# A convolution copy one tile sooner, the branch mean at tile 27, and one centring per tile, in a sparse-attention stage

## The chip, the cores and the metric

The kernel runs on one core of a Trainium2 chip. The metric is the device time of one execution in microseconds; the time before is the median of three runs. One execution was also profiled.

## The reference, cut to what matters

The program is a hybrid layer (a sparse attention with a convolution branch beside it, a cross attention, a gated feed-forward) followed by a state-space layer and a forgetting attention with their feed-forwards, for 512 tokens of width 1024 in float32. The change lies in the first part, where the attention and the branch are computed:

```python
    a_out = dsa_attention(q, k, v, qi, ki, wi)          # 8 heads of 64, 128 keys kept per query
    ga, gg = jnp.split(glu, 2, axis=-1)
    u = ga * jax.nn.sigmoid(gg)                          # 512 tokens x 512 channels
    u = causal_dwconv(u, conv_b_w, conv_b_b)             # 31 taps per channel
    b_out = jax.nn.silu(layernorm(u, ln_b_g, ln_b_b))
    x = x + jnp.concatenate([a_out, b_out], axis=-1) @ w_out
```

`layernorm` subtracts the mean over the 512 channels, then divides by the root of the mean square plus a small constant.

## The kernel before, in words

Each engine has its own program, written out by hand in the order in which it is to run; semaphores tie them together. There is no scheduler: an instruction that waits holds all that stands behind it on its engine.

The attention stage is 32 tiles, n = 8 c + t: c is one of 4 pairs of heads, t picks one of 2 heads and one of 4 query blocks of 128. For tile n TensorE makes scores (`scores`, three matmuls into a bank of FOUR, three tiles ahead), VectorE their negated maximum (`negative_max`, L2466, two tiles ahead), ScalarE the exponentials (`exponentials`, L800, two tiles ahead), TensorE turns the result (`turn`, L1798, into a bank of ACC), ScalarE copies its high part (`turned_high`, L815, into PTH), VectorE makes the low remainder (`turned_low`, L2500, into PTL, one tile behind), and TensorE multiplies with the values (`values`, L1755 to L1757, into O). In the last pair VectorE also divides each tile by its sum (`divide`, L2471 and L2473), before `turn`. In the other pairs the sums are turned on TensorE (`turn_sums`, L1891), copied by ScalarE at the next pair's t = 3 (`sums_copied`, L884, into RBs) and multiplied into the output by VectorE (`scaled_out`, L2489); `scaled_high` (L889) and `scaled_low` (L2495) split the product. `turn` of a tile with t = 3 waits for that copy.

The convolution runs beside it. Channels are in four blocks CV[0] to CV[3]. Block 0 is made by VectorE, one tap per tile (`taps`, L2373). Blocks 1 to 3 are made by TensorE as chunks of 32 steps, 4 steps in each of 8 tiles (`convolve_beside`), with diagonal weight tiles that GpSimd builds (`diagonals`, L1295), into the PSUM bank ST. There is one such bank: in the ninth tile ScalarE copies it out in four pieces and adds the bias (`convolved`, L897), and the first step of the next chunk waits for that copy (`conv_pe`). So the copies stand at tiles 8, 17 and 26.

Then comes the normalisation of the branch. TensorE sums all channels into ST (`branch_mean`, L1919, at tile 28), VectorE subtracts the mean from the four blocks (L2583, at tile 29), ScalarE squares them (`branch_square`, L903: tiles 30 and 31, and two after the loop), and GpSimd adds the squares (L1266, L1268). TensorE's `column_sums` after the first unit of the output projection wait for the last sum. The projection (`first_projected`, then `unit`, L1626, L1627, L1632) begins when tile 30's remainder is made. Its weights are loaded by SyncE into RAW, rounded by ScalarE (L627, WH) and their remainder made by GpSimd (L1255, WL), which frees the buffer for the next load.

Of the kernel before, what the change touches and what calls it, by code (L numbers as in the profile page):

```python
# [19 lines left out]
ALU = mybir.AluOpType  # L20
# [3 lines left out]
P = 128  # L24
# [10 lines left out]
BCH = 4  # L35
# [13 lines left out]
CONV_TILES = 8  # L49
CONV_CHUNKS = 3  # L50
# [76 lines left out]
def build_program(nc, A, out):  # L127
    ctx = ExitStack()
    with ctx:
        first = (nc.sbuf_base + 127) // 128 * 128  # L130

        def at(name, shape, dt, offset):
            return nc.alloc_sbuf_tensor_at(name, shape, dt, offset=first + offset)

        def bank(name):
            return ctx.enter_context(nc.psum_tensor(name, [P, 512], F32))

        def sem(name):
            return ctx.enter_context(nc.semaphore(name))
# [72 lines left out]
        CV = [at(f"CV{c}", [P, T], F32, (184320, 152576, 34816, 36864)[c]) for c in range(BCH)]  # L212
# [102 lines left out]
        def column(name, i):  # L315
# [6 lines left out]
        ST = bank("ST")  # L322
# [40 lines left out]
        u_ready, u_hi, u_lo, wc_hi, diag_ready, diag_used, conv_pe, conv_done, mean_sum, centred, ln_scaled, branch_hi, branch_lo = (  # L363
            sem(n) for n in ("u_ready", "u_hi", "u_lo", "wc_hi", "diag_ready", "diag_used",
                             "conv_pe", "conv_done", "mean_sum", "centred", "ln_scaled", "branch_hi", "branch_lo"))
# [256 lines left out]
        def _(act):  # L622
# [13 lines left out]
            def square_free(norm, c):  # L636
                if not isinstance(c, int) or SQUARES[norm] + c >= 2:
                    act.wait_ge(sq_used, SQUARES[norm] + c - 1)
# [179 lines left out]
            def out_high(kind, c, half=None):  # L818

                for m in range(1 + (kind == "cross")) if half is None else (half,):  # L820
                    chunk = bass.ds(2 * c + m if kind == "cross" else c, 1)
                    high_out((O, ST)[m], OUT[kind][0][:, chunk, :],
                             VALUES[kind] + (2 * c + m + 1 if kind == "cross" else 8 * c + 8))
# [43 lines left out]
            def high_out(bank_, to, k):  # L867

                act.wait_ge(pv_done, k)
                act.activation(to, bank_[:], ACT.Copy).then_inc(o_hi, 1)  # L870
# [8 lines left out]
            def sums_copied(kind, c, bank_):  # L879

                act.wait_ge(sums_turned, LATE[kind] + c + 1)
                if c:
                    act.wait_ge(o_scaled, LATE[kind] + c)
                act.activation(RB[kind][:], bank_[:], ACT.Copy).then_inc(sums_in, 1)  # L884
# [15 lines left out]
            def branch_square(c):  # L900
                act.wait_ge(centred, c + 1)
                square_free("ln", c)
                act.activation(SQ[:, c % 2, :], CV[c][:], ACT.Square).then_inc(sq_ready, 1)  # L903

            def attend_sparse():
                for t in range(2):
                    exponentials("sparse", t, t)
                for c in range(4):
                    for t in range(8):
                        n = 8 * c + t  # L910
                        if n + 2 < 32:
                            exponentials("sparse", n + 2, t + 2)
                        if t == 3 and c:
                            sums_copied("sparse", c - 1, TT[1])
                        turned_high("sparse", c, t)
                        if t == 4 and c:
                            scaled_high("sparse", c - 1)
                        if n % (CONV_TILES + 1) == CONV_TILES and n < CONV_CHUNKS * (CONV_TILES + 1):
                            convolved(n // (CONV_TILES + 1))
                        if n >= 30:  # L920
                            branch_square(n - 30)
                for c in range(2, BCH):
                    branch_square(c)
                out_high("sparse", 3)

            attend_sparse()

            def silu_branch(c):
# [192 lines left out]
            with act.Fori(0, 4) as i:  # L1121
                for b in range(2):
                    c = 2 * i + b
# [490 lines left out]
        def _(pe):  # L1614
# [307 lines left out]
            def attend_sparse():  # L1922
                for t in range(3):
                    scores("sparse", 0, 0, t)
                for c in range(4):
                    b = c % 2
                    for t in range(8):
                        n = 8 * c + t
                        if t + 3 < 8:
                            scores("sparse", c, b, t + 3)  # L1930
                        elif c < 3:
                            scores("sparse", c + 1, 1 - b, t - 5)
                        convolve_beside(n)
                        turn("sparse", c, t)
                        if t >= TB:
                            values("sparse", c, b, 0, BLOCKS["sparse"][t - TB])
                        elif c:
                            if t == 2:
                                turn_sums("sparse", c - 1, TT[1])
                            values("sparse", c - 1, 1 - b, 1, BLOCKS["sparse"][t])  # L1940
                        if n == 28:
                            branch_mean()

            pe.sem_inc(t_ready, 4)
# [258 lines left out]
        def _(dve):  # L2203
# [350 lines left out]

            dve.sem_inc(pt_lo, 2)

            def attend_sparse():
                def low_tile(n):
                    turned_low(n, n % 8, n % TB, keys("sparse", n % 8) // P)

                for t in range(2):
                    negative_max("sparse", t, t)
                for c in range(4):
                    for t in range(8):
                        n = 8 * c + t
                        if c == LAST["sparse"]:
                            divide("sparse", n, t)
                        if t == 0 and c:
                            inverse("sparse", c - 1)
                        if n + 2 < 32:  # L2570
                            negative_max("sparse", n + 2, t + 2)
                        if n:
                            low_tile(n - 1)
                        if t == 3 and c:
                            scaled_out("sparse", c - 1)
                        if t == 5 and c:
                            scaled_low("sparse", c - 1)
                        if n + 8 < CONVW:
                            taps(n + 8, n + 9)
                        if n == 29:  # L2580
                            dve.wait_ge(mean_sum, 1)
                            for k in range(BCH):
                                dve.scalar_tensor_tensor(CV[k][:], ST[:], -1.0 / (BCH * P), CV[k][:], ALU.mult, ALU.add)\  # L2583
                                   .then_inc(centred, 1)
                low_tile(31)
                out_low("sparse", 3)

# [444 lines left out]
            for j, to in enumerate((KT, VT)):  # L3032
                with dve.Fori(0, 4) as i:
                    for s in range(2):
                        c = 2 * i + s
                        dve.wait_ge(unit_done, START["kv"] + j * 8 + c + 1)
                        dve.tensor_tensor(to[:, bass.ds(c, 1), :], ACC[s][:], RS[:], ALU.mult).then_inc(unit_out, 1)
                    c = i + 4 * j
# [114 lines left out]
```

## Time and profile before

| | |
|---|---|
| median of 3 runs | 2074.13 us (2071.26 to 2075.82) |
| profiled execution, own time | 2074.17 us |
| its span | 2072.4 us |
| TensorE busy | 1968.3 us, 95% |
| VectorE, GpSimd, ScalarE busy | 1058.3, 1060.5, 743.8 us |
| mean granted clock of TensorE | 0.99 |

The own time is that of the execution the profile was taken of, and the span is the part of it that the profile covers. Times inside the profile are microseconds from the span's start; PE is TensorE's matmuls, PEld its weight loads, DVE VectorE, ACT ScalarE, POOL GpSimd, SP SyncE. The sparse stage's tiles run from about 188 to 286 us.

### The profile page before, as it was taken

The numbers are of one execution on the slowest core, as the hardware profiler recorded it, in microseconds if no ns is written. First come the engines' busy times: TensorE is split into PE (matmuls) and PEld (weight loads), VectorE is DVE, ScalarE is ACT, GpSimd is POOL, SyncE is SP. The second block draws the span as 40 slices with busy tenths as digits, with TensorE's granted clock in tenths as the row PEclk, the third lists the DMA queues.
The fourth block names the chain that finished last, engine by engine and source line by source line (L and its number), as shares of the span: only waits on it lengthen the run. The fifth ranks groups of instructions, "written<-read, shape, count | busy, mean of one in ns | idle before, by whom it ended". The sixth has DMA issues, their size and how long they took to land.

```text
span 2072.4 us, 31378 instructions
## 1 busy us (share of the span) xinstructions
PE 1968.3 (95%) x10733; PEld 1623.0 (78%) x10733; DVE 1058.3 (51%) x1640; ACT 743.8 (36%) x1263; POOL 1060.5 (51%) x591
## 2 busy tenths in 40 slices
PE   7989889899999999889999999999998899999997
PEld 5679867778887887667778888887878788888886
DVE  6798745835786786797442213232137724222132
ACT  4335444433213224354432222233237732222223
POOL 5576627536756645681554444456445264444442
PEclk9999999999999999999999999999999999999999
DMA  4334003143333332101233333334346333333332
GB/s 137 77 112 117 21 26 102 41 92 91 101 92 91 102 91 79 44 2 28 86 91 102 91 102 96 95 93 102 100 108 148 88 102 94 94 97 96 96 95 87
DMA packets 345028, 181.87 MB, mean 88 GB/s; under 512 B 28527, under 2 KB 336103, under 8 KB 344935
## 3 DMA queue, kind: packets, MB, share of 16 engines
q1 hardware_dynamic: 343872, 179.91, 31.3%
q8 instruction: 55, 0.90, 0.2%
q10 hardware_dynamic: 1062, 0.75, 0.1%
q14 instruction: 39, 0.31, 0.0%
HBM read 162.73 MB, written 2.10 MB: 80 GB/s over the span
## 4 chain that ended last, share of the span: by engine, by line
PE 57%; issue 12%; POOL 9%; DVE 7%; POOLq 6%; ACT 3%; DVEq 2%; SPq 2%; DMA 1%; ACTq 0%
PE ACC L1626 16%; PE ACC L1632 16%; PE ACC L1627 16%; POOL WL L1255 6%; POOLq L1269 2%; POOLq L1480 1%; POOLq L1468 1%; PE ACC L1798 1%; PE ST L2098 1%; POOL GC L1479 1%; ACT WH L627 1%; PE O L1757 1%; PE O L1755 1%; POOL GT L1467 1%; PE ST L1755 1%
## 5 line engine op out<-in xcount | busy, mean ns | idle before, releaser
L1255 POOL TENSOR_TENSOR WL<-RAW,WH 128x1024 fp32r<-128x1024 f32 (+1 forms) x292 | 692.3, 2373 | 733.4 <-ACT WH L627 677.3
L1626 PE MATMUL ACC<-PH,WH 128*128 128x512 f32 x1248 | 492.7, 395 | 8.1 <-DVE PL L2207 2.7
L1627 PE MATMUL ACC<-PL,WH 128*128 128x512 f32 x1248 | 487.3, 391 | 0.0
L627 ACT ACTIVATE WH<-RAW 128x1024 fp32r<-128x1024 f32 (+1 forms) x292 | 301.0, 1032 | 452.3 <-PE ACC L1632 403.6
L1626 PE MATMUL ACC<-QH,WH 128*128 128x512 f32 (+1 forms) x1136 | 429.6, 382 | 14.0 <-ACT WH L627 7.4
L1627 PE MATMUL ACC<-QL,WH 128*128 128x512 f32 (+1 forms) x1136 | 425.4, 379 | 0.0
L1632 PE MATMUL ACC<-PH,WL 128*128 128x512 f32 x1248 | 312.9, 393 | 0.0
L1626 PEld LDWEIGHTS ACC<-PH,WH 128*128 128x128 f32 x1248 | 235.1, 188 | 66.4 <-issue 4.9
L1632 PE MATMUL ACC<-QH,WL 128*128 128x512 f32 (+1 forms) x1136 | 270.0, 378 | 7.2 <-POOL WL L1255 3.9
L1632 PEld LDWEIGHTS ACC<-PH,WL 128*128 128x128 f32 x1248 | 234.5, 188 | 52.7 <-issue 3.6
L1627 PEld LDWEIGHTS ACC<-PL,WH 128*128 128x128 f32 x1248 | 235.1, 188 | 48.7 <-issue 1.0
L1626 PEld LDWEIGHTS ACC<-QH,WH 128*128 128x128 f32 x1136 | 214.8, 189 | 63.1 <-issue 9.2
L1627 PEld LDWEIGHTS ACC<-QL,WH 128*128 128x128 f32 x1136 | 214.8, 189 | 38.9 <-issue 0.2
L1632 PEld LDWEIGHTS ACC<-QH,WL 128*128 128x128 f32 x1136 | 205.3, 188 | 49.3 <-POOL WL L1255 5.9
L3024 DVE TENSOR_TENSOR X<-X,ACC 128x512 f32 x48 | 33.0, 688 | 216.3 <-PE ACC L1632 216.3
L3014 DVE TENSOR_TENSOR H<-ACC,RS 128x512 f32<-128x512 f32 x64 | 44.3, 692 | 149.1 <-PE ACC L1632 148.6
L1268 POOL TENSOR_TENSOR SSQ<-SSQ,SQ 128x512 f32<-128x512 f32 x51 | 75.0, 1470 | 68.1 <-ACT SQ L634 63.8
L875 ACT ACTIVATE QH<-H 128x512 f32 (+1 forms) x54 | 34.1, 632 | 158.2 <-DVE H L3016 128.3
L2500 DVE TENSOR_TENSOR PTL<-ACC,PTH 128x128 fp32r<-128x128 f32 (+2 forms) x112 | 53.3, 476 | 36.2 <-ACT PTH L815 35.8
L815 ACT ACTIVATE PTH<-ACC 128x128 fp32r<-128x128 f32 (+2 forms) x112 | 47.9, 428 | 56.6 <-PE O L1757 37.0
L875 ACT ACTIVATE PH<-H 128x512 f32 (+1 forms) x32 | 20.2, 632 | 128.3 <-DVE H L3016 128.3
L2836 DVE TENSOR_TENSOR QL<-H,QH 128x512 f32 x54 | 37.4, 693 | 49.5 <-ACT QH L875 49.5
(448 smaller groups left out, 2565.0 us busy)
## 6 DMA issues: line engine op xcount, KB each, us to landing
RAW<-in_mlp_w_dram SPq DMA_DIRECT2D x128, 512.0 KB, 4.0
RAW<-in_w_gate_dram SPq DMA_DIRECT2D x22, 512.0 KB, 3.8
RAW<-in_w_up_dram SPq DMA_DIRECT2D x22, 512.0 KB, 3.8
RAW<-in_w_in_dram SPq DMA_DIRECT2D x16, 512.0 KB, 3.9
RAW<-in_w_down_dram SPq DMA_DIRECT2D x16, 512.0 KB, 4.1
RAW<-in_ssm_w_glu_dram SPq DMA_DIRECT2D x16, 512.0 KB, 3.8
RAW<-in_w_kvf_dram SPq DMA_DIRECT2D x16, 512.0 KB, 4.0
RAW<-in_w_out_dram SPq DMA_DIRECT2D x16, 256.0 KB, 2.8
```

The source lines that it names most:

```text
L627: act.activation(WH[:, s, 0:kc], RAW[:, s, 0:kc], ACT.Copy).then_inc(w_hi, 1)
L815: act.activation(parts(kind, t // TB)[0][:, first:first + kb, qb * P:(qb + 1) * P], TT[t % 2][:, 0:kb * P].rearrange("p (k q) -> p k q", q ...
L875: act.activation(hi[:, bass.ds(k, 1), :], to, ACT.Copy).then_inc(hid_hi, 1)
L1255: pool.tensor_tensor(WL[:, s, 0:kc], RAW[:, s, 0:kc], WH[:, s, 0:kc], ALU.subtract).then_inc(w_lo, 1)
L1268: pool.tensor_tensor(SSQ[:], SSQ[:], SQ[:, s, :], ALU.add).then_inc(sq_used, 1)
L1269: pool.drain()
L1626: pe.matmul(ACC[s][:, 0:n], WH[:, s, k, :], xh[:, k, :], start=(k == 0), stop=False)
L1627: pe.matmul(ACC[s][:, 0:n], WH[:, s, k, :], xl[:, k, :], start=False, stop=False)
L1632: mm = pe.matmul(ACC[s][:, 0:n], WL[:, s, k, :], xh[:, k, :], start=False, stop=(k == kc - 1))
L1755: pe.matmul(out, ah, bh, start=first, stop=False)
L2500: dve.tensor_tensor(pair[1][to], TT[t % 2][:, 0:kb * P].rearrange("p (k q) -> p k q", q=P), pair[0][to], ALU.subtract).then_inc(pt_lo, 1)
L3014: dve.tensor_tensor(h[:], ACC[s][:], RS[:], ALU.mult).then_inc(unit_out, 1)
```

## The change

Three things. ScalarE copies the convolution result in the eighth tile of a chunk (tiles 7, 16 and 25), right behind the last convolution matmuls. TensorE sums the mean at tile 27 instead of 28. VectorE centres one block in each of tiles 28 to 31 instead of four at tile 29; the squares on ScalarE begin at tile 29 and go one per tile, and the fourth stands behind the copy of the attention output (`out_high`).

```diff
--- before.py
+++ after.py
@@ -915,13 +915,12 @@
                         turned_high("sparse", c, t)
                         if t == 4 and c:
                             scaled_high("sparse", c - 1)
-                        if n % (CONV_TILES + 1) == CONV_TILES and n < CONV_CHUNKS * (CONV_TILES + 1):
+                        if n % (CONV_TILES + 1) == CONV_TILES - 1 and n < CONV_CHUNKS * (CONV_TILES + 1):
                             convolved(n // (CONV_TILES + 1))
-                        if n >= 30:
-                            branch_square(n - 30)
-                for c in range(2, BCH):
-                    branch_square(c)
+                        if n >= 29:
+                            branch_square(n - 29)
                 out_high("sparse", 3)
+                branch_square(3)
 
             attend_sparse()
 
@@ -1938,7 +1937,7 @@
                             if t == 2:
                                 turn_sums("sparse", c - 1, TT[1])
                             values("sparse", c - 1, 1 - b, 1, BLOCKS["sparse"][t])
-                        if n == 28:
+                        if n == 27:
                             branch_mean()
 
             pe.sem_inc(t_ready, 4)
@@ -2554,6 +2553,11 @@
 
             dve.sem_inc(pt_lo, 2)
 
+            def centre(k):
+                dve.wait_ge(mean_sum, 1)
+                dve.scalar_tensor_tensor(CV[k][:], ST[:], -1.0 / (BCH * P), CV[k][:], ALU.mult, ALU.add)\
+                   .then_inc(centred, 1)
+
             def attend_sparse():
                 def low_tile(n):
                     turned_low(n, n % 8, n % TB, keys("sparse", n % 8) // P)
@@ -2577,11 +2581,8 @@
                             scaled_low("sparse", c - 1)
                         if n + 8 < CONVW:
                             taps(n + 8, n + 9)
-                        if n == 29:
-                            dve.wait_ge(mean_sum, 1)
-                            for k in range(BCH):
-                                dve.scalar_tensor_tensor(CV[k][:], ST[:], -1.0 / (BCH * P), CV[k][:], ALU.mult, ALU.add)\
-                                   .then_inc(centred, 1)
+                        if n >= 28:
+                            centre(n - 28)
                 low_tile(31)
                 out_low("sparse", 3)
 
```

How it moves instructions, at three places. Lines behind the edits are shifted by one or two in the changed kernel. The first is ScalarE at tiles 7 to 10: E and E2sparse are exponentials, PTH copied transposes, CV_132 block 1 of the convolution.

```order
 L800 ACTIVATE E,SUMF<-FOUR,NMX 128x256
 L815 ACTIVATE PTH<-ACC 128x4x128
-L800 ACTIVATE E2sparse,SUMF<-FOUR,NMX 128x384
-L815 ACTIVATE PTH<-ACC 128x128
 L897 ACTIVATE CV_132<-ST,VEC 64x256
 L897 ACTIVATE CV_132<-ST,BSW 64x256 x2
 L897 ACTIVATE CV_132<-ST,VEC 64x256
+L800 ACTIVATE E2sparse,SUMF<-FOUR,NMX 128x384
+L815 ACTIVATE PTH<-ACC 128x128
 L800 ACTIVATE E3sparse,SUMF<-FOUR,NMX 128x512
 L815 ACTIVATE PTH<-ACC 128x2x128
```

The four copies moved ahead of the exponentials of tile 10 and of tile 8's copied transposes; the other two chunks are moved in the same way.

The second is TensorE from the transposes of tile 27 on: FOUR<-KSH, KSL, SEL are the scores of tile 31, ACC<-CST,E the transposes of tile 28, O its values, ST<-CV the mean. Before:

```order
L1798 MATMUL ACC<-CST,E3sparse 128x128 x4
L1779 MATMUL FOUR<-KSH,AQ_79 128x512
L1780 MATMUL FOUR<-KSL,AQ_79 128x512
L1781 MATMUL FOUR<-SEL,PAIR 128x512
L1798 MATMUL ACC<-CST,E 128x128
L1755 MATMUL O<-PTH,VSH 128x512
L1756 MATMUL O<-PTL,VSH 128x512
L1757 MATMUL O<-PTH,VSL 128x512
L1919 MATMUL ST<-CV_131,CST 128x512
L1919 MATMUL ST<-CV_132,CST 128x512
L1919 MATMUL ST<-CV_133,CST 128x512
L1919 MATMUL ST<-CV_134,CST 128x512
```

The same place after the change:

```order
L1797 MATMUL ACC<-CST,E3sparse 128x128 x4
L1918 MATMUL ST<-CV_131,CST 128x512
L1918 MATMUL ST<-CV_132,CST 128x512
L1918 MATMUL ST<-CV_133,CST 128x512
L1918 MATMUL ST<-CV_134,CST 128x512
L1778 MATMUL FOUR<-KSH,AQ_79 128x512
L1779 MATMUL FOUR<-KSL,AQ_79 128x512
L1780 MATMUL FOUR<-SEL,PAIR 128x512
L1797 MATMUL ACC<-CST,E 128x128
L1754 MATMUL O<-PTH,VSH 128x512
L1755 MATMUL O<-PTL,VSH 128x512
L1756 MATMUL O<-PTH,VSL 128x512
```

The mean stands ahead of tile 31's scores and of tile 28's transposes and values.

The third is VectorE from tile 28's remainder to the division of tile 30 or 31: REC and E are a division, NMX a maximum, PTL a remainder, QL the low part of the scaled output, CV_131 to CV_134 the blocks that are centred. Before:

```order
L2500 TENSOR_TENSOR PTL<-ACC,PTH 128x128
L2495 TENSOR_TENSOR QL<-OFs,QH 128x512
L2583 SCALAR_TENSOR_TENSOR CV_131<-ST,CV_131 128x512
L2583 SCALAR_TENSOR_TENSOR CV_132<-ST,CV_132 128x512
L2583 SCALAR_TENSOR_TENSOR CV_133<-ST,CV_133 128x512
L2583 SCALAR_TENSOR_TENSOR CV_134<-ST,CV_134 128x512
L2471 RECIPROCAL REC<-SUM 128x1
L2473 TENSOR_SCALAR E2sparse<-E2sparse,REC 128x384
```

From tile 28's centring on, after the change:

```order
L2558 SCALAR_TENSOR_TENSOR CV_131<-ST,CV_131 128x512
L2470 RECIPROCAL REC<-SUM 128x1
L2472 TENSOR_SCALAR E<-E,REC 128x256
L2465 TENSOR_REDUCE NMX<-FOUR 128x1
L2499 TENSOR_TENSOR PTL<-ACC,PTH 128x128
L2494 TENSOR_TENSOR QL<-OFs,QH 128x512
L2558 SCALAR_TENSOR_TENSOR CV_132<-ST,CV_132 128x512
L2470 RECIPROCAL REC<-SUM 128x1
L2472 TENSOR_SCALAR E2sparse<-E2sparse,REC 128x384
L2499 TENSOR_TENSOR PTL<-ACC,PTH 128x2x128
L2558 SCALAR_TENSOR_TENSOR CV_133<-ST,CV_133 128x512
L2470 RECIPROCAL REC<-SUM 128x1
```

The first centring, with its wait for the mean, now stands ahead of tile 29's division and maximum; two centrings stand ahead of tile 30's division instead of four, and a third ahead of tile 31's.

## Rows read from the trace of the kernel before

**Rows 1.** The page, part 1: busy time, share of the span, instructions.

```profile
PE 1968.3 (95%) x10733; PEld 1623.0 (78%) x10733; DVE 1058.3 (51%) x1640; ACT 743.8 (36%) x1263; POOL 1060.5 (51%) x591
```

**Rows 2.** TensorE by stretches: length, busy time, granted clock, DMA share, GB/s.

```profile
214.30:220.00 5.70, 5.67 (x25) 0.51 0.00 0
220.00:240.60 20.60, 20.15 (x153) 1.00 0.16 39
243.80:247.10 3.30, 3.30 (x18) 0.50 0.03 5
271.90:278.00 6.10, 6.08 (x14) 0.50 0.00 0
284.60:288.10 3.50, 3.38 (x13) 0.52 0.00 0
401.80:407.00 5.20, 5.19 (x31) 1.00 0.01 3
```

**Rows 3.** Timeline of TensorE: start, us, instruction, idle before and its releaser.

```profile
214.33 0.55 PE L1755 MATMUL ST<-UH,DGH 128*128 128x256 f32 x1 [2.10 <-ACT CV L897]
...
243.01 0.36 PE L1755 MATMUL ST<-UH,DGH 128*128 128x256 f32 x1 [2.42 <-ACT CV L897]
...
271.92 1.09 PE L1798 MATMUL ACC<-CST,E3sparse 128*128 128x128 f32 x4 [2.75 <-issue]
...
283.64 0.55 PE L1798 MATMUL ACC<-CST,E2sparse 128*128 128x128 f32 x3 [2.40 <-DVE E2sparse L2473]
...
401.76 0.44 PE L1798 MATMUL ACC<-CST,E 128*128 128x128 f32 x2 [1.78 <-DVE E L2473]
```

**Rows 4.** Who writes tile CV: count, ns minimum/median/maximum, first and last start.

```profile
L2373 DVE SCALAR_TENSOR_TENSOR CV<-U,VEC,CV x30: 739/1054/2387, 173.0 to 256.4; 128x512 f32<-128x512 f32 x30
...
L897 ACT ACTIVATE CV<-ST,VEC x6: 471/478/488, 212.2 to 270.3; 64x256 f32<-64x256 f32 x6
```

**Rows 5.** Timeline of ScalarE around its copies: start, us, instruction, idle before.

```profile
208.89 0.60 ACT L815 ACTIVATE PTH<-ACC 128x512 fp32r<-128x512 f32 x1 [1.71 <-PE ACC L1798]
...
223.09 0.60 ACT L884 ACTIVATE RBs<-ACC 128x512 f32<-128x512 f32 x1
...
239.28 0.28 ACT L815 ACTIVATE PTH<-ACC 128x128 fp32r<-128x128 f32 x1 [0.99 <-PE O L1757]
...
268.40 0.49 ACT L815 ACTIVATE PTH<-ACC 128x384 fp32r<-128x384 f32 x1 [1.33 <-PE O L1757]
```

**Rows 6.** Timeline of VectorE, tiles 11 and 12, and TensorE behind it.

```profile
223.73 0.69 DVE L2489 TENSOR_TENSOR OFs<-O,RBs 128x512 f32<-128x512 f32 x1 [0.39 <-ACT RBs L884]
224.33 1.10 DVE L2373 SCALAR_TENSOR_TENSOR CV<-U,VEC,CV 128x512 f32<-128x512 f32 x1
...
226.89 0.48 PE L1755 MATMUL O<-PTH,VSH 128*128 128x512 f32 x1
```

**Rows 7.** Timeline of the mean and the end of the stage, three engines.

```profile
272.66 0.78 PE L1779 MATMUL FOUR<-KSH,AQ 128*128 128x512 f32 x1
...
275.86 4.63 PE L1919 MATMUL ST<-CV,CST 128*128 128x512 f32 x8
...
276.34 0.62 ACT L889 ACTIVATE QH<-OFs 128x512 fp32r<-128x512 f32 x1
...
277.06 0.69 DVE L2495 TENSOR_TENSOR QL<-OFs,QH 128x512 fp32r<-128x512 f32 x1 [0.29 <-ACT QH L889]
...
280.54 2.48 DVE L2583 SCALAR_TENSOR_TENSOR CV<-ST,CV 128x512 f32<-128x512 f32 x4 [2.78 <-PE ST L1919]
...
285.78 0.79 PE L1626 MATMUL ACC<-QH,WH 128*128 128x512 f32 x1
```

**Rows 8.** Timeline behind the stage: GpSimd, ScalarE, TensorE's weight load.

```profile
289.77 1.27 POOL L1268 TENSOR_TENSOR SSQ<-SSQ,SQ 128x512 f32<-128x512 f32 x1 [0.16 <-issue]
...
290.43 0.60 ACT L870 ACTIVATE QH<-O 128x512 fp32r<-128x512 f32 x1 [1.54 <-PE O L1757]
...
293.07 1.09 PEld L1646 LDWEIGHTS ST<-CST,SSQ 128*128 128x128 f32 x8
```

## The prediction, made before the changed kernel was run

> **What bounds the kernel now.** I read the page first, then TensorE's granted clock by stretches, then its idle time with the releaser named, then the engines around each hole. TensorE is busy for 95% of the span, nothing else comes near [rows 1], so a change pays only where TensorE stands still or runs slowly. The stage in question is the sparse attention with the convolution beside it, some 100 of the 2072.4 us. Between 220.0 and 240.6 TensorE is busy 20.15 of 20.60 us at clock 1.00: there it is the limit. But it stands still four times for over 2 us: 2.10 before 214.33 and 2.42 before 243.01, both released by ScalarE's convolution copy, 2.75 before 271.92, and 2.40 before 283.64, released by a VectorE division [rows 3]. After each of them stands a stretch at about half of the full clock (0.50 to 0.52, that is 1.2 of 2.4 GHz): 5.7, 3.3, 6.1 and 3.5 us [rows 2]. Half the clock means that half of such a stretch is lost. A hole of 1.78 us before 401.76 [rows 3] was followed by clock 1.00 [rows 2]. So a hole has two prices, its own length and what the clock loses behind it; shortened far enough, it saves both.
>
> The sum is made against the profiled execution: 2074.17 us, span 2072.4. The median of the runs is 2074.13, so one number serves for both.
>
> **Part A, first copy, at tile 7 instead of 8.** The copy is four instructions of 0.48 us each [rows 4], 1.95 us with the steps between them. Now it comes behind the exponentials of tile 10 and the copy of tile 8's transposes, and TensorE, whose next convolution writes the same bank, waits until 214.33. After the change it follows tile 7's transposes copy, which ends at 208.89 + 0.60 = 209.49 [rows 5]. All convolution matmuls of the chunk stand ahead of those transposes on TensorE, so the copy waits for nothing: it ends at 211.45. TensorE arrives at 214.33 - 2.10 = 212.23. The hole is gone: 2.10, and with it half of 5.7, so 2.85 [rows 2, 3]; 4.95 at most. What is late next? The exponentials of tile 10 and tile 8's copy, pushed back by 1.2 and 0.3 us (estimates from where they stand), are wanted by TensorE only at tile 10, over 3 us later. Then the chain through VectorE: from the end of the copied sums, 223.09 + 0.60 [rows 5], to the value matmuls of tile 12 at 226.89 [rows 6], it is 3.2 us: scaling 0.69, a tap 1.10, a maximum, a remainder. TensorE, 4.95 earlier, would reach its sums-dependent transposes at about 219.5, and ScalarE has the sums copied at 219.6 to 220.1, as the tap before is short or long. Plus 3.2 is 222.8 to 223.3, against 226.89: 3.6 to 4.1. I take **3.8**.
>
> Taps are the doubt in A. One takes from 739 to 2387 ns [rows 4]. With two of them at the long end the chain grows by 2 x 1.65 = 3.3 and A keeps 1.65; that is the bound from below, 4.95 the one from above. I take 3.8 because the two taps nearest to the place have 1.1 us [rows 6] and the median 1054 ns [rows 4]. The Trainium skill, page SBUF — State Buffer, section on the two separate sides, has a rule against this change: a VectorE instruction with two SBUF inputs and a GpSimd instruction that reads SBUF exclude each other for a whole instruction, so the earlier diagonal builds (they start when TensorE has used the old ones) would hold the taps. By that rule the sum for A would be the lower bound; the spread of the tap rows agrees with it. The centring is not touched by it, since one of its two inputs is PSUM.
>
> **Part B, second copy, at tile 16 instead of 17.** Here the copy follows tile 16's transposes copy, 239.28 + 0.28 = 239.56 [rows 5], and ends at 241.5. TensorE comes to the convolution at 243.01 - 2.42 = 240.59. So a hole of 1.0 us stays: 1.4 gained, and if the clock then holds, as behind the 1.78 us hole, half of 3.3, 1.65 [rows 2, 3]. Tile 17's copy and its remainder come some 0.4 us later than now; TensorE wants them at 243, and they are there. **3.0**.
>
> **Part C, third copy, at tile 25 instead of 26.** The hole before 271.92 is not made by the convolution: the transposes of tile 27 wait for the copied softmax sums, and these stand on ScalarE behind the convolution copy. ScalarE is idle for 1.33 us before 268.40 [rows 5]; the copy now fills this, so the sums come 1.2 to 1.33 earlier and TensorE resumes at 270.7. A hole of 1.55 is left. The clock is taken to hold. Its saving is inside part D.
>
> **Part D, the mean at tile 27, one centring per tile.** The mean needs the third copy (268.7) and the VectorE taps, done long ago, and ST is free. Today it takes 4.63 us [rows 7], of which until 278.0 at half clock; at full it is 4.63 - (278.0 - 275.86) / 2 = 3.55. Start 270.7, transposes 0.45, mean 3.55: the sum is there at 274.7, not at 280.5. Today VectorE then centres four blocks in 2.48 us [rows 7] ahead of tile 30's division, and TensorE goes on at 283.64 [rows 3], 3.1 after the mean. After the change one block, 0.62, stands at tile 28, another at 29. But VectorE waits for the mean a tile earlier, with tile 29's division, maximum, remainder and low part of the output queued behind. The longest way after the mean is now: TensorE's scores of tile 31 and values of tile 28, which took 275.86 - 272.66 = 3.2 at half clock with a wait in it [rows 7], so 1.5; ScalarE's copy and high part, 0.9; VectorE's low part 0.69, centring 0.62, division 0.65; hops 0.3. That is 4.65, so tile 30 goes at 279.3 instead of 283.64: 4.3 earlier. It waits some 2.3 us there, as now, and I leave the 3.5 us half-clock stretch behind it as it is. The centrings of tiles 30 and 31 put 0.3 ahead of the output projection, which begins now at 285.78 [rows 7]. C and D together **4.0**. Bounds: 5.7 if that last clock drop stays away (half of 3.5 more), 1.0 if the drop at 271.9 stays (half of 6.1 less).
>
> **Part E, squares.** The square of block 3 moves behind the output copy on ScalarE. That copy ends at 291.03; the square, 0.6, then GpSimd's add, 1.27, end at 292.9, and TensorE's column sums start their weight load at 293.07 [rows 8]. Hidden by 0.1 us. Behind it GpSimd's remainder for the second projection unit, and SyncE's load into the buffer that it frees, come 1.3 us later. I charge 0.3; bounds 0 and 1.3. No DMA is added; loads move only with the remainder that frees their buffer.
>
> **Sum:** 3.8 + 3.0 + 4.0 - 0.3 = 10.5. Everything after the stage depends on its end and only shifts. 2074.1 - 10.5 = **2063.6 us**.
>
> **Rivals.** (1) The clock falls anyway. The holes left, 1.0 and 1.55, are near the 1.78 that was harmless, and the shortest of the four harmful ones here is 2.10 [rows 3]; but TensorE is not dense around them. Price: B's 1.65 and C's 3.05 are lost, 10.5 - 4.7 = 5.8, 2068.3. Chance 0.19. (2) VectorE is the bound after A (the taps above): 10.5 - 3.8 + 1.65 = 8.35, 2065.8. Chance 0.09. (3) The change does not do what it says: TensorE finds the hole again one instruction later, at the transposes or the sums, and the parts cancel; about 2073. The dates above speak against it, at A by 0.8 us, at B by nothing to spare. Chance 0.10. (4) Slower: the copies now stand ahead of the transposes copies and exponentials of tiles 8, 17, 26. If TensorE needs these at once instead of two tiles later, ScalarE's 1.95 us go onto the path three times and the old holes are kept: 2074.1 + 5.9 = 2080.0. It decides as soon as a transposes copy is over 2 us behind TensorE's need; against it speaks that ScalarE is busy 36% [rows 1] and idle over 1 us ahead of nearly every such copy [rows 5]. Chance 0.06.
>
> **Numbers.** The forecast has 0.56. A measurement of this kernel can tell about 0.2%, 4.1 us. Forecast, (1) and (2) are faster by more: 0.84; same 0.10; slower 0.06. Range: below, the last drop gone (1.75), A in full (1.15), E nothing (0.3), 2060.4, and 0.9 for the run: 2059.5. Above, rival (1) and a little of (2): 2069.5. Some 2 in 10 lie outside.
>
> **What would show it.** In the changed profile: no TensorE idle time released by the convolution copy at tile 9, about 1 us at tile 18; clock 1.00 from there to tile 27; about 1.5 us idle before tile 27's transposes; the mean in 3.5 us, starting 5 us earlier; the wait before tile 30's transposes still over 2 us. Holes of the old length in front of transposes instead would be rival (3) or (4); clock 0.50 behind the shorter holes rival (1).

## The result, and the profile after

The changed kernel takes **2059.82 us** (median of four runs, 2059.2 to 2062.47) where the kernel before, beside it, takes 2073.31 (2071.26 to 2075.82): ratio 0.9937, 95% interval 0.9926 to 0.9949. The forecast was 2063.6 us, range 2059.5 to 2069.5. Two repeats, each beside its own runs of the kernel before, gave 0.995 (0.9937 to 0.9964) and 0.9944 (0.9932 to 0.9957). In the second, one slow execution of 2794.72 us, at a mean granted clock of 0.655, is left out. The 14 runs that are left have a median of 2061.3 us together: the gain is 11 to 12 us.

The profiled execution took 2059.2 us, span 2057.4. Page, part 1, against [rows 1]:

```profile
PE 1962.2 (95%) x10733; PEld 1617.8 (79%) x10733; DVE 1056.4 (51%) x1640; ACT 742.9 (36%) x1263; POOL 1060.0 (52%) x591
```

TensorE does the same work in 6.1 us less of busy time, and its idle time (span less busy) fell from 104.1 to 95.2 us. A stretch in which TensorE stands still is called a hole below. TensorE by stretches (length, busy time, granted clock, DMA share, GB/s), against [rows 2]:

```profile
204.00:268.00 64.00, 59.37 (x424) 1.00 0.09 22
268.00:270.00 2.00, 0.00 (x0) 0.97 0.00 0
270.00:272.00 2.00, 1.54 (x8) 0.50 0.00 0
272.00:274.00 2.00, 2.00 (x9) 0.50 0.00 0
274.00:276.00 2.00, 2.00 (x7) 0.50 0.00 0
276.00:278.00 2.00, 2.00 (x12) 0.82 0.00 0
278.00:290.00 12.00, 9.28 (x45) 1.00 0.22 66
```

Three of the four half-clock stretches are gone; one, behind tile 30's wait, is left. TensorE's timeline (start, us, instruction, idle before and its releaser), against [rows 3]:

```profile
210.78 0.33 PE L1754 MATMUL ST<-UH,DGH 128*128 128x256 f32 x1
...
235.74 0.35 PE L1754 MATMUL ST<-UH,DGH 128*128 128x256 f32 x1 [0.96 <-ACT CV L897]
...
261.59 0.63 PE L1797 MATMUL ACC<-CST,E3sparse 128*128 128x128 f32 x4 [1.32 <-issue]
262.05 3.60 PE L1918 MATMUL ST<-CV,CST 128*128 128x512 f32 x8
...
270.46 0.90 PE L1797 MATMUL ACC<-CST,E2sparse 128*128 128x128 f32 x3 [2.54 <-DVE E2sparse L2472]
...
273.23 0.79 PE L1625 MATMUL ACC<-QH,WH 128*128 128x512 f32 x1
...
281.23 0.94 PE L1645 MATMUL ST<-CST,SSQ 128*128 128x1 f32 x8
```

The hole of 2.10 at tile 9 no longer exists (the convolution's matmul at 210.78 waits for nothing), the one of 2.42 is 0.96, the one of 2.75 is 1.32, and the one at tile 30 is as long as before. ScalarE's timeline shows the copies where they now stand, and the softmax sums (RBs) behind them:

```profile
208.10 0.47 ACT L897 ACTIVATE CV<-ST,VEC 64x256 f32<-64x256 f32 x1
...
216.99 0.60 ACT L884 ACTIVATE RBs<-ACC 128x512 f32<-128x512 f32 x1
...
233.62 0.47 ACT L897 ACTIVATE CV<-ST,VEC 64x256 f32<-64x256 f32 x1
...
257.71 0.47 ACT L897 ACTIVATE CV<-ST,VEC 64x256 f32<-64x256 f32 x1
...
260.88 0.60 ACT L884 ACTIVATE RBs<-ACC 128x512 f32<-128x512 f32 x1
...
278.37 0.60 ACT L870 ACTIVATE QH<-O 128x512 fp32r<-128x512 f32 x1 [3.81 <-PE O L1756]
278.86 0.62 ACT L903 ACTIVATE SQ<-CV 128x512 f32<-128x512 f32 x1
```

**A measure of the stage that leaves the rest of the program out.** The first profile of the kernel before is 1.1 us behind that of the changed kernel already 17 us into the program, ahead of anything the change touches; a second profile of the kernel before is not. So I measure the stage by two instructions, the first matmul of the low-part scores (FOUR<-KSL) and the first scaling of the branch (CV<-CV,RS). By tile (minimum, median and maximum ns, first and last start), in the second profile of before:

```profile
L1780 PE MATMUL FOUR<-KSL,AQ x16: 273/338/628, 190.9 to 272.4; 128*128 128x128 f32 x4, 128*128 128x256 f32 x4, 128*128 128x384 f32 x4, 128*128 128x512 f32 x4
...
L2602 DVE TENSOR_TENSOR CV<-CV,RS x4: 684/685/692, 302.2 to 304.0; 128x512 f32<-128x512 f32 x4
```

and in the changed kernel:

```profile
L1779 PE MATMUL FOUR<-KSL,AQ x16: 274/310/397, 190.4 to 265.7; 128*128 128x128 f32 x4, 128*128 128x256 f32 x4, 128*128 128x384 f32 x4, 128*128 128x512 f32 x4
...
L2603 DVE TENSOR_TENSOR CV<-CV,RS x4: 684/685/691, 291.0 to 292.8; 128x512 f32<-128x512 f32 x4
```

The stage is 302.2 - 190.9 = 111.3 us before (111.4 in the first profile) and 291.0 - 190.4 = 100.6 after. TensorE's busy time and granted clock in it, before (second profile):

```profile
190.90:302.20 111.30, 96.70 (x607) 0.91 0.08 20
```

and after:

```profile
190.40:291.00 100.60, 90.80 (x607) 0.97 0.09 22
```

The same 607 matmuls are busy 5.9 us less, while the granted clock of the stage rose from 0.91 to 0.97, and the idle time is 14.60 - 9.80 = 4.8 us shorter, which is the holes. All profiles in this way; the slow clock's loss is summed from 204 to 294 over rows of 3 us as 3 x (1 - clock). A loss of 1.7 us in that sum is called a slow piece below: two of them make 3.4, six 10.2.

| kernel | stage, us | busy | idle | clock's loss | timed ratio to before |
|---|---|---|---|---|---|
| before | 111.4; 111.3 | 96.8; 96.7 | 14.6; 14.6 | 10.2; 10.2 | |
| full change | 100.6; 100.0; 98.6 | 90.8; 89.6; 88.3 | 9.8; 10.4; 10.3 | 3.4; 1.7; 0 | 0.9937; 0.995; 0.9944 |
| copies alone | 100.7 | 89.9 | 10.8 | 1.7 | 0.9948 |
| mean and centring alone | 111.5 | 96.6 | 14.9 | 10.3 | 0.9998 |
| first two copies alone | 102.3 | 91.2 | 11.1 | 3.4 | 0.9968 |
| holes filled | 107.3; 107.2 | 97.1; 95.9 | 10.2; 11.3 | 5.1; 3.4 | 0.9996; 0.9996 |
| full change, divide ahead | 103.1 | 92.5 | 10.6 | 5.1 | 0.9951 |
| copies, divide ahead | 103.4 | 92.8 | 10.6 | 5.1 | 0.995 |
| copies, divide then centre | 97.5 | 88.5 | 9.0 | 0 | 0.9929 |
| the same, third copy late | 97.2 | 88.6 | 8.6 | 0 | 0.9936 |

(The filled kernel's busy time holds its 38 spare matmuls.)

### The profile page after: what moved, and what is told of

The parts are those of the page before. It is cut to its first block, busy times and chain, and to the rows that moved or that the text cites. A ratio compares the mean times of both kernels' runs of the same rounds, so it can differ in the third digit from the quotient of the medians.

```text
span 2057.4 us, 31378 instructions
## 1 busy us (share of the span) xinstructions
PE 1962.2 (95%) x10733; PEld 1617.8 (79%) x10733; DVE 1056.4 (51%) x1640; ACT 742.9 (36%) x1263; POOL 1060.0 (52%) x591
## 4 chain that ended last, share of the span: by engine, by line
PE 57%; issue 13%; POOL 9%; DVE 7%; POOLq 6%; ACT 3%; DVEq 2%; DMA 1%; SPq 1%; ACTq 0%
PE ACC L1625 16%; PE ACC L1631 16%; PE ACC L1626 16%; POOL WL L1254 7%; POOLq L1268 2%; POOLq L1479 1%; POOLq L1467 1%; PE ST L2097 1%; PE ACC L1797 1%; POOL GC L1478 1%; ACT WH L627 1%; POOL GT L1466 1%; SPq L586 1%; DVE DS L2281 1%; PE O L1754 0%
## 5 line engine op out<-in xcount | busy, mean ns | idle before, releaser
L1625 PE MATMUL ACC<-QH,WH 128*128 128x512 f32 (+1 forms) x1136 | 429.4, 382 | 12.7 <-ACT WH L627 6.9
```

The lines of the kernel that those rows point to most:

```text
L1625: pe.matmul(ACC[s][:, 0:n], WH[:, s, k, :], xh[:, k, :], start=(k == 0), stop=False)
```

## The experiments

**Theory 1:** the copies are the change; the mean and the centring are worth little, since tile 30 waits as long as before. **Rival:** the end of the stage (parts C and D, 4.0 us of the forecast) needs the mean at tile 27.

**Copies alone.** The kernel before, with one line edited:

```diff
-                        if n % (CONV_TILES + 1) == CONV_TILES and n < CONV_CHUNKS * (CONV_TILES + 1):
+                        if n % (CONV_TILES + 1) == CONV_TILES - 1 and n < CONV_CHUNKS * (CONV_TILES + 1):
```

> The three copies one tile sooner, mean and centring where they were. Theory 1 (the moved mean and the spread centring are worth nothing: they take 1.5 us of TensorE's work out of the way before the mean and put 1.6 us of chain behind it): stage gain about 11 us against the kernel before, tile 30's transposes within 0.6 us of where the full change has them, total within 1.5 us of the full change. Theory 2 (the last part of the gain comes from the mean): stage gain of 8 to 9 us, 2 us or more behind the full change.

2061.78 us, ratio 0.9948 (0.9934 to 0.9961). TensorE's timeline:

```profile
262.14 0.63 PE L1798 MATMUL ACC<-CST,E3sparse 128*128 128x128 f32 x4 [1.33 <-issue]
...
271.86 0.55 PE L1798 MATMUL ACC<-CST,E2sparse 128*128 128x128 f32 x3 [2.40 <-DVE E2sparse L2473]
...
274.00 0.80 PE L1626 MATMUL ACC<-QH,WH 128*128 128x512 f32 x1 [0.49 <-DVE PTL L2500]
```

The same two holes as in the full change, a timed interval that overlaps its interval (0.9926 to 0.9949), and a stage 0.1 us longer than the longest of its three. Tile 30's transposes come 0.9 us later than in the full change's first profile, counted from the stage's first transposes (0.6 had been expected); by the second unit of the output projection 0.1 of that is left.

**Mean and centring alone.** The changed kernel, with the copies back at tiles 8, 17 and 26:

```diff
-                        if n % (CONV_TILES + 1) == CONV_TILES - 1 and n < CONV_CHUNKS * (CONV_TILES + 1):
+                        if n % (CONV_TILES + 1) == CONV_TILES and n < CONV_CHUNKS * (CONV_TILES + 1):
```

> Mean at tile 27 and one centring per tile, copies where they were. Theory 1: the 2.75 us hole before tile 27's transposes and the half clock behind it stay, the output projection begins within 1 us of where it does before: same. Theory 2: 2 to 3 us faster.

2072.13 us, ratio 0.9998 (0.9989 to 1.0007), with all four holes and half clock behind each:

```profile
213.15 0.55 PE L1754 MATMUL ST<-UH,DGH 128*128 128x256 f32 x1 [2.10 <-ACT CV L897]
...
242.00 0.35 PE L1754 MATMUL ST<-UH,DGH 128*128 128x256 f32 x1 [2.43 <-ACT CV L897]
...
270.91 1.08 PE L1797 MATMUL ACC<-CST,E3sparse 128*128 128x128 f32 x4 [2.75 <-issue]
...
281.16 0.90 PE L1797 MATMUL ACC<-CST,E2sparse 128*128 128x128 f32 x3 [2.54 <-DVE E2sparse L2472]
```

Theory 1 stands.

**First two copies alone.** The kernel before, with the copies at tiles 7, 16 and 26:

```diff
-                        if n % (CONV_TILES + 1) == CONV_TILES and n < CONV_CHUNKS * (CONV_TILES + 1):
+                        if n in (7, 16, 26):
```

> Only the first two copies one tile sooner. The parts add up: 4.6 + 3.0 = 7.6 us in the stage, and the 2.75 us hole before tile 27's transposes with its half clock stays. If ScalarE had become a limit through the copies, less than 6.

2065.62 us, ratio 0.9968 (0.9956 to 0.998). Tile 27's hole is as long as before:

```profile
262.74 0.87 PE L1798 MATMUL ACC<-CST,E3sparse 128*128 128x128 f32 x4 [2.74 <-issue]
```

The stage gains 9.0, which is 1.4 more than the 7.6 expected. Nearly all of that comes behind this hole, where one slow piece stands instead of two: from these transposes to tile 30's it is 10.45 us here and 11.72 before. The third copy is worth the rest: 102.3 - 100.7 = 1.6 in the profiles, 0.9968 to 0.9948 in the ratios, and 3.8 between the medians (this kernel's profile is of its fastest execution).

**Does the clock behind a hole have the price that the forecast gave it?** Spare matmuls whose results nobody reads fill the first two holes in the kernel before; nothing else moves:

```diff
+                if n in (9, 18):
+                    pe.wait_ge(pt_lo, n + 1)
+                    keep_busy(TT[n % 2], 18 + 2 * (n == 18))
```

> The kernel before, with 18 and 20 dummy matmuls of 256 columns on TensorE in the holes of tiles 9 and 18 (they write a bank that the next transposes overwrite). The holes stay as long as they are, but TensorE is busy in them. If the clock behind a hole is a price of its own: clock 1.00 from 214 to 269, gain of 2.85 + 1.65 = 4.5 us in the stage. If the slow stretches have another cause: clock 0.50 as before, no gain, or a loss of some tenths.

> The kernel before with the first two holes filled by spare matmuls, a second time, because its first profile showed a stage gain of 4.1 us and its timed median none. If the clock price behind the holes is real, the profile again shows clock 1.00 behind tiles 9 and 18 and a stage gain of 3 to 5 us; the median then stands 3 to 5 us under the kernel before only if that is not lost again later. If the price is real in the stage but the slow stretches come elsewhere instead, the profile shows a stage gain again, a loss of about as much behind the stage, and a median within 1.5 us of the kernel before. If the first profile was chance, no stage gain.

In the stage, yes, twice: the clock is 1.00 from 210 to 264, tile 27's transposes start 76.42 us after the stage's first transposes in both profiles where the kernel before needs 80.46, and the stage is 4.0 and 4.1 us shorter, against half of 5.7 and half of 3.3, 4.5 together [rows 2]. In the times, no: 2072.7 and 2072.05 us, ratio 0.9996 (0.9987 to 1.0005) both times, which leaves room for 2.7 us at most. TensorE by stretches in the second profile:

```profile
210.00:264.00 54.00, 53.08 (x404) 1.00 0.06 16
...
1507.00:1712.00 205.00, 186.77 (x1039) 0.98 0.44 111
```

The second row is the forgetting attention, which the edit does not touch. There the two profiles lose 3.4 and 5.1 us to the slow clock, where the two of before lose 1.7 each. But that does not explain the times: over everything behind the stage the first of them loses 5.1 us, as both profiles of before do, and the second 8.5, as do the first two copies alone and the first repeat of the full change, which gained in the times. Nor do the timed runs lose more to the clock: their mean granted clock is 0.9912 and 0.9916, that of the kernel before beside them 0.9896 both times, 3 to 4 us less lost over the whole program.

Behind the stage the two profiles take 2.1 and 4.7 us more than the first profile of before, the second profile of before 1.1 less; the three of the full change took 3.0 less, 2.6 more and 2.0 less. So 2.1 is within what executions differ by, and 4.7 is more than in any other profile. The price is shown where it arises, in the stage. That it counts in full in the whole program is not shown, and where the time goes is open.

**The full change again, twice.**

> The full change again, beside the next two on one chip: 10 to 15 us faster than the kernel before, 10.8 of it in the stage. If the 3 us that its first profile has outside the stage are chance, this profile shows another amount there.

> The full change once more, on the same chip and beside the same runs of the kernel before as the last arrangement. If dividing ahead of the centrings and copying the third chunk late is worth what its parts say (2.4 to 4 us and 1 us), this stands 3 to 5 us above it, at 2060 to 2063 us; if the parts are given back later, within 1.5 us of it.

2062.83 and 2058.97 us (median of five; the ratios are above). The three holes have their lengths from the first profile within 0.02 us, but the clock does not repeat. In the last one TensorE shows:

```profile
271.25 0.55 PE L1797 MATMUL ACC<-CST,E2sparse 128*128 128x128 f32 x3 [2.55 <-DVE E2sparse L2472]
```

```profile
191.20:289.80 98.60, 88.28 (x607) 1.00 0.09 22
```

and over its stage, by stretches, a clock of 1.00: the same wait, and no half clock behind it. Two slow pieces, one or none for the same program make a stage of 100.6, 100.0 or 98.6 us.

**The second profile of before.**

> The kernel before, unchanged, profiled once more. If the holes set the half-clock stretches, all four holes of over 2 us have one behind them again; outside the sparse stage the time at the same marks may differ from the first profile by up to 3 us, since the places of the other slow stretches change from one execution to the next.

2072.3 us. The four holes and the slow pieces behind them recur, 10.2 us lost both times; at 17 us the two profiles are already 1.3 us apart.

**What holds tile 30?** Its wait of 2.4 to 2.5 us survives every version so far. Theory 2: the division of tile 30 stands on VectorE behind the wait for the mean, so dividing a tile ahead frees it. Rival: the remainders in front are as late. On the full change, from tile 24 on, each tile divides the next:

```diff
-                        if c == LAST["sparse"]:
+                        if n == 24:
                             divide("sparse", n, t)
+                        if c == LAST["sparse"] and n < 31:
+                            divide("sparse", n + 1, t + 1)
```

> The full change, with the divisions of the last pair of heads one tile earlier on VectorE, so that tile 30's stands ahead of the centrings of tiles 29 and 30. If the wait before tile 30's transposes (2.54 us, and half clock behind it) is the division behind the low part of the output and the centring: the wait shrinks below 1 us, the clock holds, 2 to 4 us faster than the full change. If the remainder of tile 28 takes its place as the wait: 0.7 us at most.

And the same edit on the copies alone:

> Copies sooner and divisions one tile earlier, mean and centring as before the change (all four at tile 29). The four centrings, 2.5 us, then stand only ahead of remainders: within 1 us of the run with the full change and divisions earlier if the place of the mean does not matter, 1.5 us or more behind it if the spread centring is what lets the remainders through.

2062.74 and 2061.98 us, ratios 0.9951 (0.9938 to 0.9965) and 0.995 (0.9936 to 0.9963): nothing gained over either, and a longer stage, with three slow pieces in it. In the first, TensorE shows:

```profile
261.72 0.63 PE L1797 MATMUL ACC<-CST,E3sparse 128*128 128x128 f32 x4 [1.98 <-issue]
...
272.77 1.09 PE L1797 MATMUL ACC<-CST,E3sparse 128*128 128x128 f32 x4 [1.79 <-DVE PTL L2499]
```

```profile
273.00:276.00 3.00, 3.00 (x9) 0.50 0.00 0
```

The wait at tile 30 is gone, a new one of 1.79 stands before tile 31 on a remainder queued behind the centring (2.25 in the second kernel), and the divisions that were moved ahead everywhere enlarged tile 27's hole from 1.32 to 1.98 in both, with half clock behind it. The rival holds for this edit.

**Divide then centre.** So only the two divisions that follow the mean were moved, with the mean at tile 28 as before and one centring behind each (copies alone, and in VectorE's loop):

```diff
-                        if c == LAST["sparse"]:
+                        if 24 <= n < 30:
                             divide("sparse", n, t)
...
-                        if n == 29:
-                            dve.wait_ge(mean_sum, 1)
-                            for k in range(BCH):
-                                dve.scalar_tensor_tensor(CV[k][:], ST[:], -1.0 / (BCH * P), CV[k][:], ALU.mult, ALU.add)\
-                                   .then_inc(centred, 1)
+                        if n in (29, 30):
+                            divide("sparse", n + 1, t + 1)
+                        if n >= 29:
+                            centre(n - 29)
                 low_tile(31)
+                centre(3)
```

> Copies a tile sooner, mean at tile 28 as in the kernel before; on VectorE the division of tile 30 is made at tile 29 ahead of any centring, that of tile 31 at tile 30, and the four blocks are centred one by one behind them. Theory (the wait of 2.40 us before tile 30's transposes is the division standing behind the wait for the mean and the centrings, and nothing else is as late): that wait goes, the hole before tile 27 stays 1.3 us as with the copies alone, no half-clock stretch starts at tile 30, and the output projection starts 2.4 to 4 us earlier than with the copies alone; stage gain 13 to 15 us against the kernel before where the copies alone had 10.7; about 2058 us. Rival (the remainders of tiles 29 to 31 take the place of the division, as with the division ahead of a mean at tile 27): a wait of 1.8 us or more released by a remainder at tile 30 or 31, stage gain 9 to 11.5, about 2062 us.

2057.77 us (2056.13 to 2060.74), ratio 0.9929 (0.9916 to 0.9943). VectorE and TensorE:

```profile
266.28 0.42 DVE L2473 TENSOR_SCALAR E2sparse<-E2sparse,REC 128x384 f32<-128x384 f32 x1
267.92 0.69 DVE L2559 SCALAR_TENSOR_TENSOR CV<-ST,CV 128x512 f32<-128x512 f32 x1 [1.22 <-PE ST L1919]
```

```profile
261.31 0.63 PE L1798 MATMUL ACC<-CST,E3sparse 128*128 128x128 f32 x4 [1.33 <-issue]
...
268.47 0.49 PE L1798 MATMUL ACC<-CST,E2sparse 128*128 128x128 f32 x3
...
270.25 0.66 PE L1798 MATMUL ACC<-CST,E3sparse 128*128 128x128 f32 x4 [0.66 <-DVE E3sparse L2473]
271.32 0.50 PE L1626 MATMUL ACC<-QH,WH 128*128 128x512 f32 x1 [0.41 <-DVE PTL L2500]
```

The division is done 1.2 us before the first centring starts, and tile 30's transposes wait for nothing (268.47). The projection starts at 271.32 instead of 274.00 with the copies alone; since this profile's stage began 0.83 us earlier (first transposes at 189.87 and 190.70), that is a gain of 1.85 us, less than the 2.4 to 4 expected. The rest of the stage's gain comes behind it, where the copies alone run at half clock and this kernel does not. No slow piece is left in the stage, which is 97.5 us: 3.2 less than with the copies alone and 1.1 to 3.1 less than the full change. In the stage theory 2 stands, in the narrow form.

**Third copy late.** The hole of 1.33 before tile 27 waits for the softmax sums, and these stand on ScalarE behind the third copy, which only the mean needs. On the last kernel:

```diff
-                        if n % (CONV_TILES + 1) == CONV_TILES - 1 and n < CONV_CHUNKS * (CONV_TILES + 1):
-                            convolved(n // (CONV_TILES + 1))
+                        if n in (7, 16, 27):
+                            convolved(n // 10)
```

> The arrangement with the division ahead of the centrings, and the third copy of the convolution result moved back, from tile 25 to the end of tile 27, behind the copied softmax sums and tile 27's transposes copy. Theory (the hole of 1.33 us before tile 27's transposes is made by the third copy, 1.95 us on ScalarE, standing ahead of the sums; the third copy itself is wanted only by the mean, which comes later): the hole goes, the mean starts about 1 us earlier (0.2 to 0.3 of the 1.33 lost to waiting for the copy), stage gain about 1 us more than the same kernel with the third copy at tile 25, 15 to 15.5 us against the kernel before, median about 2057 us. Rival (the mean or tile 28's transposes copy then wait for the convolution copy): a new wait of 1 us or more at the mean or at tile 28's values, stage gain 12.5 to 14.5 us, about 2058 to 2060 us.

2058.59 us, ratio 0.9936 (0.9923 to 0.9949). TensorE:

```profile
261.07 0.63 PE L1798 MATMUL ACC<-CST,E3sparse 128*128 128x128 f32 x4 [0.77 <-issue]
...
264.35 3.67 PE L1919 MATMUL ST<-CV,CST 128*128 128x512 f32 x8
```

The hole shrank to 0.77 and no further, since ScalarE, ahead of the sums, then waits for TensorE itself. Counted from the stage's first transposes the mean starts only 0.3 us sooner (74.15 for 74.41), because the copy now ends just before it, at 264.20. That makes 0.3 us of stage where about 1 was expected: the theory missed, and stage gain and median lie in the rival's range, though its new wait did not come. Beside the second repeat of the full change, on the same runs of before, it is 0.9936 against 0.9944, intervals that overlap. It had been expected 3 to 5 us below; that repeat had no slow piece of clock, which left 98.6 - 97.2 = 1.4 us to gain. So **divide then centre** has the lowest median and a shorter stage than the change, but their timed intervals overlap too; that it is faster over the whole program is not shown.

## Why the prediction was right, point by point

The forecast, 10.5 us, meets the stage's own gain: 10.7, 11.3 and 12.7 us in the three profiles. The rest of the 15.0 us between the two first spans is not the change: 1.1 arose in the first 17 us, and what lies behind the stage came out with both signs in the repeats. The mechanism was right (shorter holes, and a clock that holds behind them), but part of the fit is luck: in the first profile A came out 0.8 too small and C with D 0.9 too large, and the two cancel. The first median lies only 0.3 us inside the range, and that of the second repeat, 2058.97, below it.

In the profile of the changed kernel the stage began 1.27 us earlier than in that of before (first transposes at 190.19 and 191.46). All differences of dates below are less this offset.

**Part A, 3.8:** too small. The value matmuls of tile 12, the date that the forecast used, came 4.7 us earlier, and tile 17's transposes 4.6. The step that failed is the date of the copied sums. The forecast let them wait for VectorE's taps and end at 219.6 to 220.1; they end at 217.59, which is 218.9 on the time scale of before, and ScalarE's last wait ahead of them is for TensorE:

```profile
216.15 0.49 ACT L815 ACTIVATE PTH<-ACC 128x384 fp32r<-128x384 f32 x1 [1.24 <-PE O L1756]
...
220.94 0.50 PE L1754 MATMUL O<-PTH,VSH 128*128 128x512 f32 x1
```

VectorE was in time. Its two taps ahead of the sums were

```profile
212.62 1.36 DVE L2372 SCALAR_TENSOR_TENSOR CV<-U,VEC,CV 128x512 f32<-128x512 f32 x1
...
214.66 0.74 DVE L2372 SCALAR_TENSOR_TENSOR CV<-U,VEC,CV 128x512 f32<-128x512 f32 x1
```

and GpSimd began the next diagonals only 0.4 us before the second of them ended:

```profile
215.02 2.15 POOL L1294 TENSOR_TENSOR DGH<-EYE,WCH 128x1024 fp32r<-128x1024 f32 x1 [1.59 <-PE ST L1756]
```

The tap behind the sums stood beside the build after that one and took 1.36 us (1.10 in the forecast), so the chain from the sums to the value matmuls was 3.35 us long, where the forecast had 3.2. By the Trainium skill, page SBUF — State Buffer, section on the two separate sides, taps and diagonal builds exclude each other. The trace agrees (a tap took 0.74 us with GpSimd idle at its start, 2.36 beside builds at 205.9). But neither of the two taps ahead of the sums was held as long as that, so the lower bound of 1.65 and rival (2) did not come true.

**Part B, 3.0:** exact in size (3.0 between tile 17's and tile 19's transposes); the hole left is 0.96 for 1.0, and the clock held behind it.

**Parts C and D, 4.0:** the dates were right, the worth of D was not. Beyond A and B, tile 27's transposes came 1.4 earlier (1.2 to 1.33 foreseen), the hole left is 1.32 (1.55), the mean took 3.6 us (3.55), and tile 30's transposes came 4.3 earlier (4.3). But with the copies alone tile 30 waits 2.40 instead of 2.54 us and comes only 0.9 later (11.0 before the first profile's date where the change has 11.9, each less its own offset), the projection 0.3 and its second unit 0.1 later. With the copies alone VectorE centres right behind the mean, all four blocks at once:

```profile
268.76 2.48 DVE L2583 SCALAR_TENSOR_TENSOR CV<-ST,CV 128x512 f32<-128x512 f32 x4 [1.78 <-PE ST L1919]
```

The step that failed is the credit: the forecast followed the end of the stage through an earlier mean, and did not work out where tile 30 goes with the mean left at tile 28. There four centrings stand ahead of its division instead of two, but nothing else of VectorE waits a tile earlier for the mean, and the two ways come out nearly alike. D alone is worth nothing measurable (0.9998); with the copies at most 100.7 - 100.0 = 0.7, at one slow piece each. From tile 30's transposes to the projection the change lost 0.63 in the first profile (0.3 foreseen): there the half clock began with these transposes, which took 0.90 us instead of 0.55 [rows 3]. By the end of the stage 3.1 of C and D's 4.0 is left.

**Part E, -0.3:** nearer nothing. The square runs behind the output copy as foreseen; the column sums start at 281.23 instead of 293.31, 12.08 earlier by the profiles' own clocks, and the third weight rounding behind them, which now waits for its load, at 285.21 instead of 297.22, 12.01 earlier. That is 0.07 lost.

**Rivals.** (1) did not come: behind 0.96 and 1.32 us the clock is 1.00 in all three profiles of the change. (3) and (4) did not: no hole of the old length came up anywhere else, and the one that the third copy makes before tile 27, 1.32, is the one foreseen in C. For the last drop, left as it was in the forecast, both cases occurred, and they span most of the difference between the three stage gains.

## What to carry to other kernels

In this stage a hole on TensorE cost its own length and what the clock lost behind it; the second part was the larger, 5.9 to 8.4 us of busy time in a stage gain of 10.7 to 12.7. So price both and read the granted clock row by row, but time the whole program too: saving the clock alone, by filling two holes, shortened the stage by 4 us and the program by nothing measurable. Put a copy that frees a bank right behind the last matmul that fills it, but try each part of such a change by itself: here the one-line edit of the copies did it all. When several parts of an engine's program wait for one late event, move what does not need the event ahead of the wait, and only that; moving more made another hole longer.

## What was not expected of the hardware

The clock's losses in the stage took few values. They were 10.2, 10.2 and 10.3 us in the kernels with all four holes open, and 0, 1.7, 3.4 or 5.1 in all others. How many slow pieces there are is not fixed by the holes: a wait of 2.54 or 2.55 us before tile 30 was followed by two, one and none in three executions of one program. Nor does the length of a hole tell by itself: the forecast's harmless hole of 1.78 us before 401.76 was followed by clock 1.00 [rows 2], but behind the 1.79 us before tile 31 with the divisions ahead the clock is 0.50 from 273 to 276. In TensorE's busy time a piece cost less than 1.7: 88.3, 89.6 and 90.8 us in the three executions, 1.3 and 1.2 each; and 96.7 - 88.3 = 8.4 for the six of the kernel before, 1.4 each. Taking holes away cut the losses in every version tried; keeping TensorE busy through two of them cut the losses in the stage and not the measured time.
